# The second expert stage in plain float32: 96 slots in three lots of 32, four column groups

## The chip, the cores and the metric

The kernel runs on one core of a Trainium2 chip. The metric is the device time of one execution in microseconds (us), the median of three runs. A measurement of this kernel tells a change from none from about 0.2% on. Engines are named as in the profile: PE is TensorE, PEld its weight loads, DVE is VectorE, ACT is ScalarE, SP is SyncE, which issues nearly all DMAs.

## The reference, cut to what matters

256 tokens of width 1024 pass a first block (mixers and 32 experts) and a second block of two layers. The last layer ends with a mixture of 8 experts, two per token, and a per-layer embedding. The change is in this mixture:

```python
def swiglu(x, w1, w3, w2):
    return (jax.nn.silu(x @ w1) * (x @ w3)) @ w2

def moe_swiglu(x, router_w, router_b, w1, w3, w2):
    logits = (x @ router_w + router_b).astype(jnp.float32)
    top_v, top_i = lax.top_k(logits, TOP_K)                  # TOP_K = 2 of N_EXPERTS_2 = 8
    top_p = jax.nn.softmax(top_v, axis=-1)
    gate = jnp.sum(jax.nn.one_hot(top_i, N_EXPERTS_2, dtype=jnp.float32) * top_p[..., None], axis=-2)
    gate = gate.astype(x.dtype)
    out = jnp.zeros_like(x)
    for e in range(N_EXPERTS_2):
        out = out + gate[..., e:e + 1] * swiglu(x, w1[e], w3[e], w2[e])
    return out
```

x is 256x1024 in float32, w1 and w3 are 1024x2816 for each expert, w2 is 2816x1024. That is 8 x 3 x 1024 x 2816 x 4 bytes = 276.8 MB of weights. With the given inputs the reference sends 81, 47, 76, 46, 65, 81, 65 and 51 tokens to the eight experts.

## The kernel before, in words

**Streaming.** SP streams all weights of the kernel, in the order of use, into a ring of nine pieces (RAW = 9) of at most 2048 floats on each of 128 partitions, 1 MB. `stream` (L535) lets piece n go only when piece n - 9 is used up (semaphore `used`, incremented by the last matmul on a piece).

**Precision.** In most stages a weight piece is first split in two fp32r parts: ACT casts it to an upper part (`split_high`, L657, into `high_parts`), DVE subtracts to get the lower part in place (`split_low`, L661). The left operand is split too, and each product takes three fp32r matmuls (`matmul3`, L624 to L626; `lower_last`, L634, L635, L638). The first expert stage (moe1, `pairs_pe`, L2748) does otherwise: it multiplies the raw float32 pieces, with two experts of 64 slots each side by side as two column groups of 64 columns of the array (L2830, L2845).

**The second expert stage (moe2, `moe_main_pe`, L2368, with `moe_main_act` and `moe_main_dve`).** Each expert has one bucket of 128 slots; four buckets make a group (TOGETHER = 4). DVE makes one-hot selections (L2642), PE gathers the rows of a group with them (L2374, L2377), gathers each slot's gates, and turns the selections. The width 2816 is walked in steps of 512 and one of 256: 6 steps an expert, 48 in all. A step has four up pieces (two of w1, two of w3; 4 rows of 512 floats a partition) and two down pieces (2 rows of w2 of 1024 floats), so the stage has 264 MB-pieces in 280 DMAs. For a step PE does up (L634, L635, L638; banks 2 and 3), ACT the silu (L2584), DVE the product with the gate (L2676), PE turns the hidden block (L2425), ACT and DVE evacuate it in two parts (L2559, L2661), PE does down (L624 to L626; banks 0 and 1). down of a step is issued behind up of the next. After an expert ACT and DVE take its result in two parts (L2566, L2665), PE scatters it to the tokens in four quarters (L2439, L2440), DVE adds them to x (L2682). For the last expert the two halves of the columns are taken one after the other (L2627, L2736, L2629, L2738), so that the first half is out before the last matmuls are done.

**What stands around it.** Before the stage: the output projection of the mixer, the router and its norm; the ring already holds the first nine pieces of moe2, and ACT and DVE have split three of them. After it: `ple_part(1)` with five pieces, then the final norm and the stores. If an expert has more tokens than its cap (128 before), `rest_pe` and its like run a general loop (`overfull`); otherwise they are jumped over.

## Time and profile before

| | |
|---|---|
| median of 3 runs (lowest, highest) | 2231.16 us (2228.6, 2231.96) |
| the profiled execution | 2228.87 us |
| its span, first to last instruction | 2227.1 us |
| PE, PEld, DVE, ACT busy | 94%, 70%, 62%, 50% of the span |
| bytes moved | 617.42 MB, mean 277 GB/s |

The page's section 2 cuts the span in 40 slices of 55.7 us, each digit tenths of busy time. The first expert stage fills slices 7 to 14, the second slices 26 to 39. Durations of matmuls are modelled and overlap; the pace of a stretch is read from starts: (start of the last minus start of the first) over the count.

### The profile page before, as it was taken

The page shows a single profiled execution, that of the slowest core. Times are in us where ns is not written, and L with a number is a line of the kernel's source. Part 1 is how long each engine was busy: PE and PEld are TensorE (multiplying, and loading weights), DVE is VectorE, ACT ScalarE, POOL GpSimd, SP SyncE. Part 2 cuts the span into 40 slices and gives each one's busy share as a digit, 9 for nine tenths or more (in the row PEclk, how much of TensorE's full clock was granted, in tenths as well). Part 3 has the DMA queues.
Part 4 walks back from the last instruction along what each step waited for, and adds up shares of the span by engine and source line. Part 5 has one row for each costly group of instructions (what it writes and reads, how often), then busy time and mean ns, then how long its engine had stood idle before and what let it go on. Part 6 is the DMA issues. An engine that isn't in the chain of part 4 may idle for free.

```text
span 2227.1 us, 28497 instructions
## 1 busy us (share of the span) xinstructions
PE 2095.3 (94%) x11674; PEld 1548.8 (70%) x11674; DVE 1369.9 (62%) x1689; ACT 1113.0 (50%) x1267; POOL 24.9 (1%) x35
## 2 busy tenths in 40 slices
PE   9999989889777889999999989999999999999997
PEld 7678873234222258778888877888888888888885
DVE  8766661011000037765546767888898888989886
ACT  6545431000000035564336546667777676777765
POOL 1000000000000000100000010000000000000000
PEclk9999999999999999999999999999999999999999
DMA  9754448999999986165555522699999989999991
GB/s 224 199 151 152 152 142 349 421 422 421 421 421 421 421 316 223 36 209 183 170 175 189 168 78 91 245 364 359 368 357 365 363 294 363 358 372 357 367 358 47
DMA packets 281497, 617.42 MB, mean 277 GB/s; under 512 B 31880, under 2 KB 130440, under 8 KB 243984
## 3 DMA queue, kind: packets, MB, share of 16 engines
q1 hardware_dynamic: 279952, 611.85, 76.4%
q10 hardware_dynamic: 1408, 3.67, 0.4%
q8 instruction: 95, 1.56, 0.3%
q14 instruction: 42, 0.34, 0.1%
HBM read 612.34 MB, written 1.05 MB: 275 GB/s over the span
## 4 chain that ended last, share of the span: by engine, by line
PE 74%; DMA 15%; DVE 6%; ACT 3%; issue 1%; SPq 0%; POOL 0%; DVEq 0%; ACTq 0%; POOLq 0%
PE ps L634 9%; PE ps L635 9%; PE ps L638 9%; PE ps L624 8%; PE ps L626 8%; PE ps L625 8%; DMA ring<-in_w_up 5%; DMA ring<-in_w_down 5%; DMA ring<-in_w_gate 4%; PE ps L2830 4%; PE ps L2845 1%; DVE ring_parts L661 1%; ACT high_parts L657 1%; PE ps L2040 1%; PE ps L2047 1%
## 5 line engine op out<-in xcount | busy, mean ns | idle before, releaser
L661 DVE TENSOR_TENSOR ring_parts<-ring,high_parts 128x2048 fp32r<-128x2048 f32 (+2 forms) x382 | 854.7, 2272 | 127.0 <-ACT high_parts L657 126.0
L657 ACT CAST high_parts<-ring 128x2048 fp32r<-128x2048 f32 (+2 forms) x382 | 716.8, 1899 | 101.0 <-PE ps L626 53.7
L626 PE MATMUL ps<-high_parts,arena_parts 128*128 128x512 f32 (+1 forms) x860 | 339.4, 395 | 0.0
L2830 PE MATMUL ps<-ring,arena 128*64 128x512 f32 x1024 | 232.4, 596 | 51.6 <-DMA ring<-in_w_up 26.6
L634 PE MATMUL ps<-high_parts 128*128 128x512 f32 x528 | 208.6, 395 | 0.0
L2830 PEld LDWEIGHTS ps<-ring,arena 128*64 128x64 f32 x1024 | 80.1, 136 | 184.7 <-issue 184.5
L635 PE MATMUL ps<-high_parts 128*128 128x512 f32 x528 | 206.1, 390 | 0.0
L624 PE MATMUL ps<-high_parts,hT_parts 128*128 128x512 f32 (+1 forms) x480 | 195.0, 406 | 0.0
L626 PEld LDWEIGHTS ps<-high_parts,arena_parts 128*128 128x128 f32 x860 | 162.0, 188 | 39.0
L625 PE MATMUL ps<-ring_parts,hT_parts 128*128 128x512 f32 (+1 forms) x480 | 188.4, 392 | 0.0
L634 PE MATMUL ps<-high_parts,hT_parts 128*128 128x512 f32 (+1 forms) x448 | 176.9, 396 | 0.8 <-ACT arena L1360 0.8
L624 PE MATMUL ps<-high_parts,arena_parts 128*128 128x512 f32 x380 | 150.9, 397 | 1.6 <-DVE arena_parts L2661 1.0
L625 PE MATMUL ps<-ring_parts,arena_parts 128*128 128x512 f32 x380 | 150.6, 396 | 0.0
L3002 DVE SCALAR_TENSOR_TENSOR arena<-ps,arena 128x512 f32<-128x512 f32 x16 | 12.0, 750 | 215.6 <-PE ps L2830 199.1
L638 PE MATMUL ps<-ring_parts,high_parts 128*128 128x512 f32 x528 | 141.5, 390 | 0.0
L2845 PE MATMUL ps<-ring,arena 128*64 128x512 f32 x512 | 116.5, 596 | 26.1 <-DMA ring<-in_w_down 25.4
L2918 ACT COPY arena<-ps 128x512 f32<-128x512 f32 x16 | 9.4, 586 | 252.3 <-PE ps L2797 252.3
L638 PE MATMUL ps<-ring_parts,hT_parts 128*128 128x512 f32 (+1 forms) x448 | 119.7, 389 | 0.7 <-DVE ring_parts L661 0.7
L638 PEld LDWEIGHTS ps<-ring_parts,high_parts 128*128 128x128 f32 x528 | 99.1, 188 | 21.2
L634 PEld LDWEIGHTS ps<-high_parts 128*128 128x128 f32 x528 | 99.5, 189 | 19.9
L635 PEld LDWEIGHTS ps<-high_parts 128*128 128x128 f32 x528 | 99.2, 188 | 20.2
L635 PE MATMUL ps<-high_parts,arena_parts 128*128 128x512 f32 (+1 forms) x292 | 113.0, 388 | 0.0
(615 smaller groups left out, 2776.9 us busy)
## 6 DMA issues: line engine op xcount, KB each, us to landing
ring<-in_moe_w SPq DMA_DIRECT2D x248, 1024.0 KB, 5.5
ring<-in_w_gate SPq DMA_DIRECT2D x64, 1024.0 KB, 16.1
ring<-in_w_up SPq DMA_DIRECT2D x64, 1024.0 KB, 16.1
ring<-in_w_down SPq DMA_DIRECT2D x64, 1024.0 KB, 16.6
ring<-in_w_in SPq DMA_DIRECT2D x104, 256.0 KB, 4.7
ring<-in_ffn_w SPq DMA_DIRECT2D x44, 512.0 KB, 4.9
ring<-in_w_in SPq DMA_DIRECT2D x20, 1024.0 KB, 5.8
ring<-in_moe_w SPq DMA_DIRECT2D x32, 512.0 KB, 5.0
```

The source lines that it names most:

```text
L624: pe.matmul(dst, a_hi, b_hi, start=first, stop=False, skip_group_check=True)
L625: pe.matmul(dst, a_hi, b_lo, start=False, stop=False, skip_group_check=True)
L626: return pe.matmul(dst, a_lo, b_hi, start=False, stop=last, skip_group_check=True)
L634: pe.matmul(dst, x_hi, w_hi, start=first and i == 0, stop=False, skip_group_check=True)
L635: pe.matmul(dst, x_lo, w_hi, start=False, stop=False, skip_group_check=True)
L638: mm = pe.matmul(dst, x_hi, w_lo, start=False, stop=last and i == len(x) - 1, skip_group_check=True)
L657: act.copy(high_flat(p), raw_flat(p)).then_inc(upper, 1)
L661: dve.tensor_tensor(raw_flat(p, ring_parts_flat), raw_flat(p), f32(high_flat(p)), ALU.subtract).then_inc(split, 1)
L2040: pe.matmul(ps[:, 2 * t + h, :], x_hidT[:, t, c, :], a[:, c, cols], start=(k == 0 and c == 0), stop=False, skip_group_check=True)
L2047: mm = pe.matmul(ps[:, 2 * t + h, :], x_hidT_lo[:, t, c, :], a[:, c, cols], start=False, stop=(k == f.steps - 1 and c == FB // P - 1), ski ...
L2830: mm = pe.matmul(ps[rows, bank, :], pair_rows[r][:, c0 + i, q * P + a * HALF:q * P + (a + 1) * HALF], w[a][:, i, :], start=(c0 + i == 0), ...
L2845: mm = pe.matmul(ps[rows, half, :], pair_hidT[:, c, rows], w[a][:, i, half * 512:(half + 1) * 512], start=(st.j == 0 and c == 0), stop=(st ...
```

## The change

`plan_moe` and `moe_main_*` go; `plan_wide`, `wide_pe`, `wide_act` and `wide_dve` come for moe2:

- The cap is 96 slots an expert, as three lots of 32 (LOTS, SPAN). Selections, gathered rows and turned selections are 384 wide instead of 512.
- No piece of moe2 is split, in the stage or ahead of it, and nor are the gathered rows and the hidden block. Matmuls take the raw float32 ring.
- A step is 1024 wide (the last of an expert 768): 3 steps an expert, 24 in all, with eight up pieces (2 rows of 1024 or 768 floats a partition) and four or three down pieces. There are 280 DMAs as before: 216 of 1 MB, 64 of 768 KB.
- In `up` and `down` the stationary operand is 128x32 (a lot), the moving one 256 or 192 columns. Four matmuls in a row take the four quarters of the 1024 columns, each in its own column group of the array, so a piece has 2 x 3 x 4 = 24 matmuls. Lot g's gate half and up half lie in bank 2 + g.
- The hidden block is turned by DVE in 32x32 blocks (`dve.transpose`), not by PE. The gate no longer goes into the hidden block: it scales the result, in twelve instructions of 32x256 (six on ACT, six on DVE), which also bring the quarters into rows of slots. `gates` therefore makes every slot's gates on all four column groups (96 small matmuls for a group of four experts).
- The result of the last expert is no longer taken in halves during its last matmuls; both engines wait for the last piece.

The diff, its core:

```diff
 PAIRS, HALF = NE1 // 2, P // 2
+LOTS, SPAN = 3, 96
...
+        def plan_wide(name, w1, w3, w2, gain_row):
...
+            f.subs, f.e, f.cap, f.passes, f.buckets = NE2, 1, SPAN, 2, NE2
+            f.base, f.plan = dict(moe_before), []
+            f.rows_before = KC
...
+            starts = range(0, DFF, 1024)
+            for b in range(f.buckets):
+                rows = w2[b]
+                for k, c0 in enumerate(starts):
+                    st = Step()
+                    st.bucket, st.c0, st.n, st.since = b, c0, min(1024, DFF - c0), k
...
+            def down(st):
+                rows = w2[st.bucket][st.c0:st.c0 + st.n].rearrange("(p c) n -> p c n", p=P)
+                return [new_piece([(0, PIECE, rows[:, c:c + 2, :])]) for c in range(0, st.n // P, 2)]
+
             for s, st in enumerate(f.plan):
                 st.own, st.no = s + 1, f.base["step"] + s + 1
-                st.up = gu_pieces_of(f, st.e, st.c0, st.n)
+                cols = slice(st.c0, st.c0 + st.n)
+                st.up = [new_piece([(0, 2 * st.n, w[st.bucket][:, c:c + 2, cols])]) for w in (f.w1, f.w3) for c in range(0, KC, 2)]
                 if s:
-                    q = f.plan[s - 1]
-                    q.down = down_pieces_of(f, w2, q.e, q.c0, q.n)
-            q = f.plan[-1]
-            q.down = down_pieces_of(f, w2, q.e, q.c0, q.n)
-            first = 0
-            for s, st in enumerate(f.plan):
-                if st.first:
-                    first = s
-                st.since = s - first
+                    f.plan[s - 1].down = down(f.plan[s - 1])
...
-            if half and f is moe2:
-                act.wait_ge(used, pieces_of["out_1_2"][-1].n + 1)
-                split_high(act, f.plan[0].up[2])
...
-                pe.wait_ge(split, p.k)
-                a, b = high_of(p, D), low_of(p, D)
...
-                    mm = matmul3(pe, ps[:, half, :], m_hidT[:, c, :], m_hidT_lo[:, c, :], a[:, i, cols], b[:, i, cols],
-                                 st.first and c == 0, st.last and c == st.n // P - 1)
...
+            def gates(r):
+                for c in (KC - 2, KC - 1):
+                    rows_ready(pe, f, r, c)
+                for q in range(TOGETHER):
+                    for g in range(LOTS):
+                        at, e = SPAN * q + 32 * g, TOGETHER * r + q
+                        for t in range(NT):
+                            for s in range(4):
+                                mm = pe.matmul(ps[32 * s:32 * s + 32, 5, 6 * q + 2 * g:6 * q + 2 * g + 2], f32(wide_sel[:, t, at:at + 32]),
+                                               gate_w[:, t, 2 * e:2 * e + 2], start=(t == 0), stop=(t == NT - 1), skip_group_check=True)
+                mm.then_inc(sig("moe_gates_psum"), 1)
...
+            def up(st, i):
+                p, r, q = st.up[i], st.bucket // TOGETHER, st.bucket % TOGETHER
+                off, n = (0, 256)[i // 4], st.n // 4
+                pe.wait_ge(piece_ready[p.slot], p.ready)
+                w = raw_flat(p).rearrange("p (c n) -> p c n", n=st.n)
+                for k in range(2):
+                    c = 2 * (i % 4) + k
+                    if st.first and q == 0 and i < 4:
+                        rows_ready(pe, f, r, c)
+                    for g in range(LOTS):
+                        x_rows = wide_rows[r][:, c, q * SPAN + 32 * g:q * SPAN + 32 * g + 32]
+                        for s in range(4):
+                            mm = pe.matmul(ps[32 * s:32 * s + 32, 2 + g, off:off + n], x_rows, w[:, k, s * n:(s + 1) * n],
+                                           start=(i == 0 and k == 0), stop=(i % 4 == 3 and k == 1), skip_group_check=True)
+                mm.then_inc(used, 1)
+
+            def down(st, i):
+                p = st.down[i]
+                if i == 0:
+                    pe.wait_ge(sig("moe_hidT"), st.no)
+                    if st.first and st.bucket:
+                        pe.wait_ge(sig("moe_y"), base + st.bucket)
+                pe.wait_ge(piece_ready[p.slot], p.ready)
+                w = raw_flat(p).rearrange("p (c n) -> p c n", n=D)
+                hidT = wide_hidT[st.no % 2][:, 0:LOTS * st.n // 4].rearrange("p (g j t) -> p g j t", g=LOTS, t=32)
+                final = st is f.plan[-1] and i == len(st.down) - 1
+                for k in range(2):
+                    j = 2 * i + k
+                    for g in range(LOTS):
+                        for s in range(4):
+                            mm = pe.matmul(ps[32 * s:32 * s + 32, g // 2, g % 2 * 256:g % 2 * 256 + 256], hidT[:, g, j, :],
+                                           w[:, k, 256 * s:256 * s + 256], start=(st.first and j == 0 and g != 1),
+                                           stop=(st.last and j == st.n // P - 1), skip_group_check=True)
+                            if final and (k, g, s) == (1, LOTS - 1, 1):
+                                mm.then_inc(sig("moe_half_done"), 1)
+                mm.then_inc(used, 1)
+
+            held = None
...
+                if held:
+                    pe.wait_ge(sig("moe_hid"), held.no)
+                for i in range(8):
+                    up(st, i)
+                    if i == 3 and s == 0:
+                        pe.wait_ge(*ended("moe2_gates"))
+                        gates(0)
+                    if i == 3 and k == 0 and b == TOGETHER - 1:
+                        gates(1)
+                    if 2 <= i < 6 and k == 1 and b:
+                        scatter(b - 1, i - 2)
+                    if i == 5 and k == 1 and b % TOGETHER == 0:
+                        turn_sel(b // TOGETHER)
+                if held:
+                    for i in range(len(held.down)):
+                        down(held, i)
+                if k == 2 and b == TOGETHER - 2:
+                    gather(1)
+                held = st
...
+            def result(b):
+                act.wait_ge(used, f.plan[3 * b + 2].down[-1].n + 1)
+                act.wait_ge(sig("moe_scattered"), 4 * (base + b))
+                for s in range(2):
+                    for g in range(LOTS):
+                        ins = act.mul(wide_y[32 * g:32 * g + 32, 256 * s:256 * s + 256],
+                                      ps[32 * s:32 * s + 32, g // 2, g % 2 * 256:g % 2 * 256 + 256],
+                                      wide_gate[32 * s:32 * s + 32, wide_scale(b, g, 0)])
+                astep(act, ins)
+                ins = act.copy(m_yh[0:SPAN, 0:512], wide_y[0:SPAN, 0:512])
+                ins.then_inc(*((sig("moe_half_upper"), 1) if b == f.buckets - 1 else (sig("moe_y_upper"), 1)))
+                act.wait_ge(sig("wide_y"), b + 1)
...
+            def silu(st):
+                act.wait_ge(used, st.up[-1].n + 1)
+                if st.own > 1:
+                    act.wait_ge(sig("moe_hid"), st.no - 1)
+                n = st.n // 4
+                for g in range(LOTS):
+                    ins = act.activation(wide_sg[:, g * n:g * n + n].rearrange("p (j i) -> p j i", i=32),
+                                         ps[:, 2 + g, 0:n].rearrange("p (i j) -> p j i", i=32), ACT.Silu,
+                                         scale=wide_gate[:, wide_scale(st.bucket, g, 1)])
+                ins.then_inc(sig("moe_silu"), 1)
...
+                for s in range(2, 4):
+                    for g in range(LOTS):
+                        ins = dve.tensor_scalar(wide_y[32 * g:32 * g + 32, 256 * s:256 * s + 256],
+                                                ps[32 * s:32 * s + 32, g // 2, g % 2 * 256:g % 2 * 256 + 256],
+                                                wide_gate[32 * s:32 * s + 32, wide_scale(b, g, 0)], None, ALU.mult)
+                ins.then_inc(sig("wide_y"), 1)
...
+            def product(st):
+                dve.wait_ge(used, st.up[-1].n + 1)
+                dve.wait_ge(sig("moe_silu"), st.no)
+                if st.own > 1:
+                    dve.wait_ge(sig("moe_hidT"), st.no - 1)
+                n = st.n // 4
+                hid, hidT = wide_hid[:, 0:LOTS * n], wide_hidT[st.no % 2][:, 0:LOTS * n]
+                dve.tensor_tensor(hid.rearrange("p (g j i) -> p g j i", g=LOTS, i=32),
+                                  ps[:, 2:2 + LOTS, 256:256 + n].rearrange("p g (i j) -> p g j i", i=32),
+                                  wide_sg[:, 0:LOTS * n].rearrange("p (g j i) -> p g j i", g=LOTS, i=32), ALU.mult)\
+                    .then_inc(sig("moe_hid"), 1)
+                dve.wait_ge(sig("moe_hid"), st.no)
+                dve.transpose(hidT, hid).then_inc(sig("moe_hidT"), 1)
...
-                    if l and i == 1:
-                        act.wait_ge(used, pieces_of[name][1].n + 1)
-                        split_high(act, moe2.plan[0].up[0])
-                        split_high(act, moe2.plan[0].up[1])
...
-            stage_moe(moe2),
+            stage_wide(moe2),
```

`select`, `gather`, `turn_sel`, `scatter`, `rows`, `gate`, `add` and the order of `wide_act` and `wide_dve` follow `pairs_*` and `moe_main_*`, with 96 for 128.

## Rows read from the trace of the kernel before

**Rows 1.** The page: busy time, and the span in 40 slices.

```profile
PE 2095.3 (94%) x11674; PEld 1548.8 (70%) x11674; DVE 1369.9 (62%) x1689; ACT 1113.0 (50%) x1267; POOL 24.9 (1%) x35
...
PE   9999989889777889999999989999999999999997
...
GB/s 224 199 151 152 152 142 349 421 422 421 421 421 421 421 316 223 36 209 183 170 175 189 168 78 91 245 364 359 368 357 365 363 294 363 358 372 357 367 358 47
```

**Rows 2.** Waits of PE, 1420 to 2181 us: us, times, longest.

```profile
PE ps L624 <- DVE arena_parts L2661: 1.0, 1, 1.0
PE ps L624 <- DVE ring_parts L661: 0.6, 1, 0.6
```

**Rows 3.** Groups by form, 1400 to 2227 us: count, busy us, mean ns.

```profile
L661 DVE TENSOR_TENSOR ring_parts<-ring,high_parts 128x2048 fp32r<-128x2048 f32 x267 | 597.3, 2284 | 18.1 <-ACT high_parts L657 18.1
L657 ACT CAST high_parts<-ring 128x2048 fp32r<-128x2048 f32 x266 | 501.2, 1915 | 58.8 <-PE ps L638 37.0 <-PE ps L626 21.8
...
L2584 ACT ACTIVATE arena<-ps,arena 128x256 f32<-128x256 f32 x8 | 3.8, 476 | 10.3 <-PE ps L638 10.3
```

**Rows 4.** Timeline of PE, first up piece: start us, us, form, count.

```profile
1403.57 0.39 PE L634 MATMUL ps<-high_parts,hT_parts 128*128 128x512 f32 x1
...
1406.31 0.39 PE L634 MATMUL ps<-high_parts,hT_parts 128*128 128x512 f32 x1
```

**Rows 5.** Timeline of PE, float32 product in four column groups (L3763).

```profile
922.90 1.50 PE L3763 MATMUL ps<-ring,arena 128*32 128x128 f32 x44
```

**Rows 6.** The same line: ns min, median, max.

```profile
L3763 PEld LDWEIGHTS ps<-ring,arena x128: 106/110/110, 922.9 to 1323.3; 128*32 128x32 f32 x128
L3763 PE MATMUL ps<-ring,arena x128: 272/273/297, 922.9 to 1323.4; 128*32 128x128 f32 x128
```

**Rows 7.** Timeline of PE in the first expert stage, a pair of pieces.

```profile
537.37 3.65 PE L2830 MATMUL ps<-ring,arena 128*64 128x512 f32 x16 [0.66 <-DMA ring<-in_w_up]
```

**Rows 8.** Busy time by stretch: us, engines, granted clock, DMA share, GB/s.

```profile
1420.00:2180.00 760.00, 758.30 (x3394) 624.91 (x3393) 660.65 (x407) 544.10 (x379) 0.00 (x0) 1.00 0.98 354
520.00:760.00 240.00, 193.71 (x852) 71.79 (x850) 22.03 (x29) 14.86 (x21) 0.00 (x0) 1.00 1.01 421
1415.00:1419.00 4.00, 4.00 (x28) 3.61 (x27) 0.00 (x0) 0.00 (x0) 0.00 (x0) 1.00 1.05 398
```

**Rows 9.** Timelines, first expert stage: SP first reissue, PE last pair.

```profile
342.05 1.33 SPq L535 DMA_DIRECT2D ring<-in_w_gate  x2
...
802.36 3.65 PE L2845 MATMUL ps<-ring,arena 128*64 128x512 f32 x16 [1.28 <-DMA ring<-in_w_down]
```

**Rows 10.** Timeline of PE before and in the gather of the second stage.

```profile
1392.02 0.40 PE L1763 MATMUL ps<-r_pairs,causal_up 128*128 128x16 f32 x2 [1.75 <-DVEq L1932]
...
1394.18 0.79 PE L2374 MATMUL ps<-arena_parts 128*128 128x512 f32 x1
...
1395.20 0.63 PE L2374 MATMUL ps<-arena_parts 128*128 128x512 f32 x1
1395.63 0.63 PE L2377 MATMUL ps<-arena_parts 128*128 128x512 f32 x1
...
1399.12 0.41 PE L2374 MATMUL ps<-arena_parts 128*128 128x512 f32 x1
1399.36 0.40 PE L2377 MATMUL ps<-arena_parts 128*128 128x512 f32 x1
```

**Rows 11.** Timeline of PE at the second stage's end.

```profile
2181.54 0.40 PE L626 MATMUL ps<-high_parts,arena_parts 128*128 128x512 f32 x1
2181.99 0.50 PE L2439 MATMUL ps<-arena_parts 128*128 128x512 f32 x1
```

**Rows 12.** Timelines of DVE, then ACT, at the second stage's end.

```profile
2181.24 0.69 DVE L2736 TENSOR_TENSOR arena_parts<-ps,arena_parts 128x512 fp32r<-128x512 f32 x1 [2.50 <-ACT arena_parts L2627]
...
2183.20 2.47 DVE L2682 TENSOR_TENSOR x<-x,ps 128x512 f32<-128x512 f32 x4
...
2185.93 1.58 ACT L820 ACTIVATE hT_parts<-ps,l_gT 128x256 fp32r<-128x256 f32 x4
```

More of the change, by code:

```diff
@@ L433, in plan_moe @@
+            moe_before["group"] += f.buckets // TOGETHER
             f.until = order["piece"]
             f.adds = 4 * moe_before["bucket"]
-            f.subs, f.cap, f.passes = buckets, P, 1
-            plan_rest(f, width)
+            plan_rest(f, DFF)
             return f
@@ L1963, in emit @@
         lot = [MX.take(PIECE) for _ in range(HIGH)]
-        moe2.group.high = [lot[k] for k in (2, 1, 0, 3, 4)]
         MX = Arena(arena)
@@ L1967, in emit @@
         pair_rows = [MX.take(KC, TOGETHER * P) for _ in range(2)]
+        MX.at = HI_AT
+        wide_rows = [MX.take(KC, TOGETHER * SPAN) for _ in range(2)]
+        wide_sg, wide_hid = MX.take(LOTS * 256), MX.take(LOTS * 256)
+        wide_hidT = [MX.take(LOTS * 256) for _ in range(2)]
+        wide_y = MX.take(D)
         assert MX.at <= HI_END
+        wide_gate = arena[:, MR_AT:MR_AT + 48]
+        wide_sel = m_sel.rearrange("p t n -> p (t n)")[:, 0:NT * TOGETHER * SPAN].rearrange("p (t n) -> p t n", t=NT)
         MX.at = MR_AT + MR_SIZE + 1024
@@ new lines, in wide_scale, with wide_act, rows, gate @@
+        def wide_scale(b, g, what):
+            at = 24 * (b // TOGETHER) + 6 * (b % TOGETHER) + 2 * g + what
+            return slice(at, at + 1)
+        def wide_act(act, f):
+            base = f.base["bucket"]
+            def rows(r):
+                for c in range(0, KC, 2):
+                    act.wait_ge(sig("moe_gathered"), KC * (f.base["group"] + r) + c + 1)
+                    act.copy(wide_rows[r][:, c, :], ps[:, 5 + c % 3, 0:TOGETHER * SPAN]).then_inc(sig("moe_rows_upper"), 1)
+            def gate(r):
+                act.wait_ge(sig("moe_gates_psum"), f.base["group"] + r + 1)
+                act.copy(wide_gate[:, 24 * r:24 * r + 24], ps[:, 5, 0:24]).then_inc(sig("moe_gates"), 1)
+            def result(b):
[10 more added lines that the diff above has]
+                act.wait_ge(sig("wide_y"), b + 1)
+                act.copy(m_yh[0:SPAN, 512:D], wide_y[0:SPAN, 512:D]).then_inc(sig("moe_y_upper"), 1)
+            def turned_sel(r):
+                act.wait_ge(sig("moe_sel_turned"), f.base["group"] + r + 1)
+                act.copy(m_selT[0:SPAN].rearrange("p b s -> p (b s)"), ps[0:SPAN, 5:7, :].rearrange("p a b -> p (a b)"))\
+                    .then_inc(sig("moe_selT"), 1)
+            def silu(st):
[8 more added lines that the diff above has]
+                ins.then_inc(sig("moe_silu"), 1)
+            router_exp_act(act, f)
+            rows(0)
+            for s, st in enumerate(f.plan):
+                b, k = st.bucket, st.since
+                if s == 1:
+                    ahead = act.mark_branch_hint_location()
+                if k == 0 and b == TOGETHER - 1:
+                    rows(1)
+                    gate(1)
+                if s == 0:
+                    gate(0)
+                if k == 1 and b:
+                    result(b - 1)
+                if k == 1 and b % TOGETHER == 0:
+                    turned_sel(b // TOGETHER)
+                if s == 0:
+                    act.wait_ge(sig("moe_gates"), f.base["group"] + 1)
+                if k == 0 and b == TOGETHER:
+                    act.wait_ge(sig("moe_gates"), f.base["group"] + 2)
+                silu(st)
+            rest_act(act, f, ahead)
+            result(f.buckets - 1)
+            rows_upper(act, 1)
+            split_until(act, "act", group_ple[1], 1)
@@ L3043, in moe_gained_dve, with stage_wide @@
+        def stage_wide(f):
+            return (lambda pe: wide_pe(pe, f)), (lambda act: wide_act(act, f)), (lambda dve: wide_dve(dve, f)), no_pool
         def moe_gained_dve(dve, f, half):
```

495 lines of the change are left out of this document (129 added, 366 removed).

## The prediction

> **What bounds the kernel now.** I read the page first, then the stage of the change by stretches, then its waits, then its timelines. The page shows PE at 94% and GB/s at 421 in slices 7 to 13 but near 360 in slices 26 to 38 [rows 1]. So the first expert stage runs at the speed of the DMAs and the second does not. The stretches say the same: from 1420 to 2180 us PE is busy 758.3 of 760 us at a granted clock of 1.00 and 354 GB/s flow; from 520 to 760 us 421 GB/s flow and PE has gaps [rows 8]. In the second stage PE waited 1.6 us in all [rows 2]. The splits on DVE (597 us from 1400 us on) and ACT (501 us) are large, but PE never stands for them, so taking them away is worth nothing by itself [rows 3]. What sets the end there is the pace of PE: the first up piece takes 1403.57 to 1406.31, 2.74 us for 12 matmuls [rows 4]. A piece of 1 MB at 421 GB/s takes 2.49 us. The stage runs from 1403.57 us to the last down matmul, which ends at 2181.94 us [rows 4, 11], 778.4 us for 276.8 MB, where 421 GB/s would need 657 us.
>
> **PE after.** A piece gets 24 matmuls of 128x32 by 256 columns. The nearest form is L3763: raw float32 of the ring, 128x32 stationary, 128 columns, four column groups in turn. 44 of them take 1.50 us [rows 5], the last being 0.27 us long [rows 6], so (1.50 - 0.27) / 43 = 28.6 ns each, 114 ns for four. The first expert stage has 16 matmuls of 512 columns in two column groups in 3.65 us, at most 456 ns a pair [rows 7]. Both give 0.89 ns a column with all groups at work. Four of 256 columns are then 228 ns, 57 ns each, and a piece 24 x 57 = 1.37 us, against 2.74. A bound below is the 28.6 ns of [rows 5] (0.7 us), one above is serial work, taken up under the rivals. At 1.37 us PE is far ahead of a piece every 2.49 us. The stage turns from PE to the DMAs, as the first expert stage is.
>
> A page of the Trainium skill speaks against this: "FP8 and Floating Point Precision", TensorE Precision Notes, has true FP32 take four passes through the array. By it 256 columns cost 1024 cycles, 427 ns for four, and a piece would need 2.56 us, just over a DMA's pace. The trace disagrees: by four passes a pair of 512 columns would be 853 ns, and [rows 7] has 456 at most.
>
> **DMAs after.** All nine slots are free or filling, since PE waits for data. SP starts to refill when the first piece is used. Nine of the 280 pieces lie in the ring by then. Of the rest 119 are up pieces of 1 MB in rows of 4 KB, 64 are of 768 KB in rows of 3 KB, 88 are down pieces in rows of 8 KB. The first expert stage has rows of 8 KB at 421 GB/s [rows 8]. That is 311 ns a row on each of 16 DMA engines. In the second stage, in a short stretch with only up pieces in rows of 2 KB, 398 GB/s flow [rows 8], 82 ns a row. Between them by a straight line, 4 KB take 158.6 ns (413 GB/s, 2.54 us a piece) and 3 KB 120.5 ns (408 GB/s, 1.93 us). Sum: 119 x 2.538 + 64 x 1.928 + 88 x 2.491 = 302.0 + 123.4 + 219.2 = 644.6 us. The bounds are 421 GB/s throughout (635 us) and the worse of the 2 KB figures, 354 GB/s of the long stretch, for all up pieces (about 703 us; but there PE held the DMAs back, so I take the line). The first expert stage shows what is lost beside this: from SP's first refill at 342.05 to PE's last pair at 802.36 are 460.3 us [rows 9], where 183 pieces at 2.49 make 455.8. The difference, 4.5 us, is the way from issue to landing and small gaps; I add it.
>
> **Start.** The gather before the stage takes 1394.18 to 1403.57, 9.4 us [rows 4, 10]. With 384 columns for 512 it is three quarters, 7.0 us, and PE starts up at 1401.2. The selection ahead of it is on DVE and only gets narrower. The splits that fall away from ACT and DVE before the router are not what the gather waits for; I give them nothing. SP's first refill is at 1401.2 + 1.4 = 1402.6. The 96 gate matmuls stand behind the fourth piece, 2.7 us at 28.6 ns; the ring and the queue ahead hide them, as they hide the second gather (about 6 us), the turned selections (2 us) and the scatters (64 matmuls of 0.24 us in the whole stage). None of these holds PE longer than the some 20 us that eight pieces in flight cover. If that cover were gone, they would cost some 30 us together.
>
> **End.** The last piece can be used at 1402.6 + 644.6 + 4.5 = 2051.7, its matmuls end 1.6 us later, 2053.3. Before this was 2181.94: 128.6 us gained. Behind it the change adds. Before, the first half of the result was ready by then: the scatter starts at 2181.99 and the adds at 2183.20 [rows 11, 12]. After, ACT must do six products of 32x256 and a copy, and DVE a subtraction. The nearest row is four 128x256 activations in 1.58 us, 0.39 us each [rows 12], so 2.35 + 0.6 + 0.7 and two hand-overs make 3.8 us; a bound below is 2 us (half the rows' time, being 32 partitions), one above 6 us (the 0.48 us of the silu [rows 3] and slow hand-overs). Of these 3.8 the second half saves about 0.6, as its subtraction follows at once. I take +3.2 us. The five pieces of the last embedding are no longer in the ring when the stage ends; they land some 3 to 15 us after the last piece, while the scatters, the turning of x and its norm run, so they stay hidden, with a few us at risk.
>
> **Other parts.** The silu is three instructions of 128x256, 0.48 us each [rows 3], then a product of 768 elements a row (1 to 1.5 us by the 0.69 us of 512 elements [rows 12]) and the turn in 32x32 blocks, which no row shows: between 0.5 and 5 us. The next up waits only for the product, about 3 us after the last up piece. Four down pieces, 10 us of data, lie between. The turn is needed another eight pieces later. So all of it is worth 0. The waits of `result` on ACT stand ahead of a silu, but a whole up lies before that silu's data. The cap of 96 is not reached: the fullest expert has 81 tokens, so the general loop stays out.
>
> **Sum.** 128.6 - 3.2 = 125.4 us. The profiled execution of 2228.87 us becomes 2103.5; the median of the runs, 2231.16, lies 2.3 higher and becomes **2106 us**. Bounds of the unknown terms: DMA 421 throughout, -10; the up rows at 398 instead of 413 and 408, +16; more if slots are refilled in bursts; the tail -2 to +10. Own range 2090 to 2135.
>
> **Rivals.**
> - *A matmul costs about 108 ns, not 57.* Either float32 costs nearly twice what I read, or the clock falls from 2.4 to 1.2 GHz because PE now stands half of the time. For it: at 1395.20 matmuls that later come every 0.24 us come every 0.43 [rows 10], after PE stood 1.75 us; that is 1.8 times; the new gaps are 1.1 us after each 1.4 us of work. Against it: gaps of 0.66 us leave the granted clock at 1.00 [rows 7, 8]. PE's work: 264 MB-pieces x 24 x 0.108 = 684 us and 30 of the small work, from 1401.2 to 2115, so 62 us over the forecast: 2168 us.
> - *Slower: weight loads don't overlap.* Each matmul brings its own load of 128x32, 110 ns long [rows 6]. Place: the 6720 matmuls of `up` and `down`. From 111 ns a matmul on the kernel gets slower (the 778 us of the stage less 30, over 6720). Load and matmul end to end are 164 ns: about 1100 us for the stage, some 2560 us in all; loads alone one after the other, 770 us, 2223. Against it: in [rows 5] four matmuls, with four loads of 110 ns, take 114 ns, so loads of different groups do overlap. The Trainium skill, "TensorE: Matmul & The Clock Gate", Part 3, says that loads overlap running matmuls only where the row group differs, and here all share the rows; by that rule this rival is the forecast, at 164 ns. [Rows 5] shows the same layout without such a stall.
> - *The DMAs stay at the old pace.* With 4 KB rows no better than 354 GB/s the stage needs 58 us more: 2164. Against it: 398 in a short stretch with shorter rows.
> - *The change does not do what it says*: the general loop runs for an expert over 96. With 81 at most it can't; it would cost hundreds of us.
>
> **How the numbers follow.** Forecast 0.77; matmul of 108 ns 0.08; DMAs at the old pace 0.06; other stalls of 30 to 60 us 0.03; weight loads 0.05 (nearly all slower); general loop 0.01. A measurement tells 0.2% from no change. Faster: 0.77 + 0.08 + 0.06 + 0.03 = 0.94; slower 0.05; same 0.01. The own range leaves a little out on both sides; with part of the two middle rivals (a clock or a rate that fails for part of the stage) I set 2090 to 2150.
>
> **What would show it.** Stretches from 1420 to 2040 us at 412 to 416 GB/s; PE waiting for the DMAs in most pieces; 24 matmuls of a piece starting within 1.4 us; SP's waits gone to the landing side, with landings near 20 us; the last piece's matmuls at 2052 us; 48 us from there to the end. Wrong would be matmuls every 108 ns or more, a granted clock under 0.9, GB/s under 400 with PE waiting, or a wait of PE for `moe_hid` or `moe_y`.

## The result, and the profile after

The changed kernel takes 2198.76 us (median of four runs, 2195.8 to 2200.63) against 2231.56 of the kernel before beside it: a ratio of 0.985, interval 0.9835 to 0.987. So it is faster, by 33 us and not by the 125 us forecast. The sign was right, the size was not, and 2199 lies outside the range of 2090 to 2150.

The profiled execution took 2200.63 us with a span of 2198.8. Its page has these lines: busy time of each engine, PE and GB/s in 40 slices, and the DMA queue that the profile names `instruction` (transfers, MB, share of the engines' time).

```profile
PE 2051.8 (93%) x22118; PEld 1415.1 (64%) x22118; DVE 789.4 (36%) x1408; ACT 615.3 (28%) x1009; POOL 24.9 (1%) x35
...
PE   9999989879777889999999999999999999999997
...
GB/s 221 200 147 147 155 161 305 421 421 421 421 422 421 421 359 271 4 203 171 172 187 196 155 98 78 152 307 412 369 385 350 320 403 369 408 382 377 412 363 68
...
q8 instruction: 176, 2.88, 0.5%
```

Beside [rows 1], DVE fell from 1370 to 789 us and ACT from 1113 to 615. PE fell only from 2095 to 2052 and is still full in every slice of the stage. The GB/s touch 412 in two slices and lie mostly under it. The number of PE instructions went up from 11674 to 22118. The forecast had 24 matmuls a piece, 6720 in the stage. The groups of PE by form, 1400 to 2150 us (count, busy us, mean ns, idle us before), show another number:

```profile
L2744 PE MATMUL ps<-ring,arena 128*32 128x256 f32 x6144 | 349.9, 384 | 6.7 <-DVE arena L2924 3.7 <-issue 3.0
L2762 PE MATMUL ps<-ring,arena 128*32 128x256 f32 x4224 | 235.0, 379 | 0.5 <-issue 0.5
L2744 PE MATMUL ps<-ring,arena 128*32 128x192 f32 x3072 | 127.6, 326 | 1.5 <-issue 1.5
```

`up` (L2744) has 128 pieces of 1 MB with 24 matmuls each, 3072, and the trace has 6144. `down` (L2762) has 88 x 24 = 2112, and the trace has 4224. **One plain float32 matmul is two records.** The timeline of PE at the stage's start (start us, us, form, count) gives the pace:

```profile
1403.25 0.40 PE L2676 MATMUL ps<-arena_parts 128*128 128x384 f32 x1
1403.58 10.57 PE L2744 MATMUL ps<-ring,arena 128*32 128x256 f32 x192
1413.97 0.90 PE L2702 MATMUL ps<-gate_w,arena_parts 128*32 128x2 f32 x83
1415.54 1.05 PE L2702 MATMUL ps<-gate_w,arena_parts 128*32 128x2 f32 x107 [0.68 <-issue]
```

Four pieces take 1403.58 to 1413.97, 10.4 us: 192 records every 54 ns, or 96 matmuls every 108 ns, 2.60 us a piece. The forecast had 1.37 us for it, the kernel before 2.74 [rows 4]. The waits of PE in the stage and just behind it, 1395 to 2165 us (total us, times, longest), hold no DMA:

```profile
PE ps L2744 <- issue: 4.6, 4, 3.0
PE ps L2702 <- issue: 4.5, 2, 3.8
PE ps L2728 <- DVE arena_parts L2909: 4.4, 1, 4.4
PE ps L2744 <- DVE arena L2924: 3.7, 1, 3.7
PE ps L2711 <- DVE x L2934: 0.8, 1, 0.8
```

And the stretches (us, busy us of PE, PEld, DVE, ACT, POOL, granted clock, DMA share, GB/s):

```profile
1420.00:2140.00 720.00, 708.69 (x13389) 489.44 (x13392) 95.07 (x138) 60.46 (x136) 0.00 (x0) 0.99 0.97 370
...
1500.00:1520.00 20.00, 20.00 (x380) 14.34 (x375) 0.00 (x0) 0.44 (x2) 0.00 (x0) 1.00 1.02 412
```

In the whole stage 370 GB/s flow, against 354 in [rows 8]. Where only up and down pieces run, it is 412. The last `down` ends at 2147.68 us. So the stage is 744.1 us long, where it was 778.4; the rest up to the span's end is 51.1 us, where it was 45.2 (2227.1 less 2181.9).

### The profile page after: what moved, and what is told of

Read it like the earlier page. It is cut to its first block, busy times and chain, and to the rows that moved or that the text cites. A ratio compares the mean times of both kernels' runs of the same rounds, so it can differ in the third digit from the quotient of the medians.

```text
span 2198.8 us, 48386 instructions
## 1 busy us (share of the span) xinstructions
PE 2051.8 (93%) x22118; PEld 1415.1 (64%) x22118; DVE 789.4 (36%) x1408; ACT 615.3 (28%) x1009; POOL 24.9 (1%) x35
## 4 chain that ended last, share of the span: by engine, by line
PE 73%; DMA 15%; DVE 6%; ACT 3%; issue 2%; SPq 0%; POOL 0%; DVEq 0%; ACTq 0%; POOLq 0%
PE ps L2744 21%; PE ps L2762 10%; DMA ring<-in_w_up 5%; DMA ring<-in_w_down 5%; PE ps L622 5%; PE ps L624 5%; PE ps L623 5%; DMA ring<-in_w_gate 4%; PE ps L2451 4%; PE ps L632 2%; PE ps L633 2%; PE ps L636 2%; PE ps L2466 1%; PE ps L2041 1%; PE ps L2048 1%
## 5 line engine op out<-in xcount | busy, mean ns | idle before, releaser
L2744 PE MATMUL ps<-ring,arena 128*32 128x256 f32 (+1 forms) x9216 | 477.6, 365 | 8.3 <-issue 4.6
L2744 PEld LDWEIGHTS ps<-ring,arena 128*32 128x32 f32 x9216 | 328.2, 111 | 148.1 <-issue 21.1
L659 DVE TENSOR_TENSOR ring_parts<-ring,high_parts 128x2048 fp32r<-128x2048 f32 (+2 forms) x118 | 264.2, 2245 | 108.1 <-ACT high_parts L655 107.2
L2762 PE MATMUL ps<-ring,arena 128*32 128x256 f32 x4224 | 235.0, 379 | 0.5 <-issue 0.5
L655 ACT CAST high_parts<-ring 128x2048 fp32r<-128x2048 f32 (+2 forms) x118 | 219.3, 1864 | 39.4 <-PE ps L624 29.1
L2762 PEld LDWEIGHTS ps<-ring,arena 128*32 128x32 f32 x4224 | 154.6, 110 | 74.6 <-issue 1.3
L624 PE MATMUL ps<-high_parts,arena_parts 128*128 128x512 f32 (+1 forms) x508 | 199.9, 393 | 0.0
L622 PE MATMUL ps<-high_parts,hT_parts 128*128 128x512 f32 (+1 forms) x480 | 194.7, 406 | 0.0
L623 PE MATMUL ps<-ring_parts,hT_parts 128*128 128x512 f32 (+1 forms) x480 | 188.3, 392 | 0.0
L633 PE MATMUL ps<-high_parts,arena_parts 128*128 128x512 f32 (+1 forms) x292 | 113.0, 388 | 0.0
L632 PE MATMUL ps<-high_parts,hT_parts 128*128 128x512 f32 (+1 forms) x272 | 107.4, 396 | 0.8 <-ACT arena L1358 0.8
L622 PEld LDWEIGHTS ps<-high_parts,hT_parts 128*128 128x128 f32 x480 | 90.7, 189 | 21.1 <-issue 2.2
L623 PEld LDWEIGHTS ps<-ring_parts,hT_parts 128*128 128x128 f32 x480 | 90.6, 189 | 18.8
```

What stands on the lines that cost most here:

```text
L622: pe.matmul(dst, a_hi, b_hi, start=first, stop=False, skip_group_check=True)
L623: pe.matmul(dst, a_hi, b_lo, start=False, stop=False, skip_group_check=True)
L624: return pe.matmul(dst, a_lo, b_hi, start=False, stop=last, skip_group_check=True)
L632: pe.matmul(dst, x_hi, w_hi, start=first and i == 0, stop=False, skip_group_check=True)
L633: pe.matmul(dst, x_lo, w_hi, start=False, stop=False, skip_group_check=True)
L655: act.copy(high_flat(p), raw_flat(p)).then_inc(upper, 1)
```

## The experiments

The theory after the result (A): TensorE still sets the pace, since a float32 matmul costs 108 ns here and the small work between the pieces comes on top of it. The rival (B): the DMAs, now close to their bound, set it. The first four kernels tell these apart.

**Matmuls alone.** A program with one line for each kind of matmul, operands in SBUF, no DMA while it runs:

```diff
+for k in range(48):          # L51, and L54 with one group only
+    for s in range(4):
+        pe.matmul(ps[32*s:32*s+32, 1, 0:256], w[:, 0, lot(k)], w[:, 1, 256*s:256*s+256], ...)
+for k in range(48):          # L57 in float32, L60 in fp32r
+    pe.matmul(ps[:, 3, 0:256], w[:, 0, block(k)], w[:, 1, 0:256], ...)
```

> A program of TensorE work alone, on operands that lie in SBUF; it computes nothing of the reference. Blocks of matmuls, each with a line of its own: after a warm-up, 192 plain float32 matmuls (128x32 stationary by 256 columns) dealt over the four column groups; 48 of the same in one group; 48 of 128x128 by 256 in float32; the same in the rounded type; 128x128 by 512 in the rounded type; 192 with 2 columns in four groups; then groups of 24 float32 matmuls with 2 or with 4 matmuls of 96x128 by 512 in the rounded type after them. Theory A, two records for each float32 matmul at the pace that the changed kernel shows: the first block shows 384 records at 54 ns, 20.8 us, and the groups work side by side, so the second takes four times as long for each matmul (430 ns, 48 in 20.7 us), and so does 128x128 by 256 in float32; the rounded type takes a quarter of that (108 ns), and 512 columns 215 ns. The changed form then costs as much for 96 slots (3 lots x 4 groups x 108 ns = 1.30 us for a chunk of 128x1024 weights) as the form before did for 128 (3 parts x 2 x 215 = 1.29 us). Theory B, a matmul is one record of 54 ns and the rest of the time is waiting: 192 records in 10.4 us. A change between the two forms costs 0.2 to 0.3 us each way by the scatters' rows in the changed kernel; the rival is that it costs nothing and the scatters were waiting for something else.

Its timeline of PE (start us, us, form, count, idle before):

```profile
24.87 20.93 PE L51 MATMUL ps<-w 128*32 128x256 f32 x384
45.61 20.88 PE L54 MATMUL ps<-w 128*32 128x256 f32 x96
66.43 20.99 PE L57 MATMUL ps<-w 128*128 128x256 f32 x96
87.06 6.10 PE L60 MATMUL ps<-r 128*128 128x256 f32 x48
93.00 11.07 PE L63 MATMUL ps<-r 128*128 128x512 f32 x48
104.00 2.30 PE L67 MATMUL ps<-w 128*32 128x2 f32 x255
108.90 1.89 PE L67 MATMUL ps<-w 128*32 128x2 f32 x128 [2.61 <-issue]
...
119.09 2.80 PE L72 MATMUL ps<-w 128*32 128x256 f32 x48
121.82 0.73 PE L74 MATMUL ps<-r 96*128 96x512 f32 x2
122.48 2.80 PE L72 MATMUL ps<-w 128*32 128x256 f32 x48
```

All float32 lines show two records a matmul, the rounded type (fp32r) one. 192 matmuls in four groups take 20.7 us (24.87 to 45.61), 108 ns each; 48 in one group take 20.8 us, 434 ns each. So the groups do run side by side, four times as fast. But the full 128x128 form in float32 takes 430 ns, no more than the one group (L57), and fp32r 124 ns for the same 256 columns (L60) and 229 ns for 512 (L63), where 108 and 215 were expected. Per block of 128x1024 weights the new form costs 3 lots x 4 groups x 108 = 1.30 us, the old one 3 parts x 2 x 229 = 1.37 us. **Three quarters of the slots at four times the work of one rounded pass is three passes again: the change trades three for three.** Expected were 1.30 and 1.29.

The period of the last lines is 122.48 - 119.09 = 3.39 us. Without 2.60 for the float32 part and 0.46 for two fp32r matmuls, 0.33 us are left: a change of form and back costs that.

The two-column matmuls (L67) start some 8 ns apart for 255 records; then PE pauses 2.6 us with no releaser, though no weights flow here, and 128 records later 2.1 us more. With the pauses the 384 records take 8.9 us (104.00 to 112.90), 23 ns each. **The traces say what these pauses end with.** In this program a transfer of 16 KB in the queue `instruction` starts at 106.55 us and one at 110.50, and PE goes on at 108.90 and 112.90, 2.4 us after each. In the stage of the change it is the same: such transfers at 1413.33, 1418.72 and 1699.16 us, PE goes on at 1415.54, 1420.93 and 1701.54. In the traces of the change, its repetition and four of its variants below (all but two lots) there are 32 places in the stage where PE starts nothing for over 0.45 us with no releaser, and each ends 2.2 to 2.6 us after the start of such a transfer; with the two here it is 34 of 34. The transfers come every 6.7 us in the stage, so chance would hardly do it. On the average one of them brings 125 records with their weight loads (22118 records, 176 transfers); at 54 ns a record these last 6.8 us, at 8 ns 1 us. So PE very likely waits for its own instructions, which many tiny matmuls use up faster than they come; no experiment changes the supply of instructions alone.

The Trainium skill, "FP8 and Floating Point Precision", TensorE Precision Notes, counts four passes for true FP32, and this agrees: 434 ns is 3.8 times the 114 ns that half a matmul of 512 columns has (229 / 2), and 3.5 times the 124 ns of 256 columns. It is the rule that the prediction set aside. The skill's "TensorEngine Tiling (Array Packing)", Key Properties, says that a change of the tiling mode drains the engine. The 0.33 us are what a change of form and back costs here; the forms differ in data type and in the size of the stationary operand too, and no run tells how much of it is the drain.

**Two lots of three.** Only the range of the loop over the lots in `up` and `down` is changed, from 3 to 2.

```diff
-                    for g in range(LOTS):
+                    for g in range(2):
```

> The changed kernel without the third lot's matmuls in up and down: slots 64 to 95 of each expert are not computed. Everything else, the transfers too, stays. Theory A (TensorE at 48 records of 54 ns a piece, 2.60 us, sets the pace): a piece falls to 32 records, 1.73 us, under the 2.55 us in which the 16 queues bring 1 MB at 412 GB/s. The stage of 744 us then becomes that of the transfers, 276.8 MB at 412 GB/s = 672 us and a few us of start: 2125 to 2140 us. Theory B (the transfers set the pace already, TensorE only waits for them): no gain, 2190 to 2201 us. If the small work between the pieces (scatters, gates, gather, the first wait for VectorE) were added to either, the gain would be under 45 us.

2132.83 us, ratio to before 0.956 (0.9547 to 0.9579): 66 to 67 us under the change. That is A, and B is out. PE now waits for the DMAs as the forecast said of the change itself (waits of the whole span, then two stretches):

```profile
PE ps L2744 <- DMA ring<-in_moe_w: 69.3, 119, 2.1
PE ps L2762 <- DMA ring<-in_moe_w: 49.1, 74, 2.2
```

```profile
1420.00:1440.00 20.00, 16.29 (x280) 10.38 (x276) 1.94 (x2) 2.48 (x4) 0.00 (x0) 0.94 0.85 301
...
1520.00:1560.00 40.00, 30.76 (x568) 17.02 (x561) 3.58 (x5) 2.24 (x6) 0.00 (x0) 1.00 1.02 410
```

This kernel is what I had forecast: a TensorE ahead of its data. Its stage lasts 675 us, from 1404.76 us, where 652.1 were forecast. The rate was nearly right, 409 to 412 GB/s for 413. But in the first 35 us only about 290 flow, since PE stands 4.7 us at the gates and 3.7 us in the second step, which costs some 10 us. From 1440 to 2080 us the mean is 408, where the forecast's sum (267.4 MB in 644.6 us) stands for 415; that is 11 more. So even with the pace that I took, the forecast was some 23 us too low in the stage.

**Half the data.** Each piece brings one of its two chunks, and both products use that one:

```diff
-... w[st.bucket][:, c:c + 2, cols] ...     rows[:, c:c + 2, :]     w[:, k, ...]
+... w[st.bucket][:, c:c + 1, cols] ...     rows[:, c:c + 1, :]     w[:, 0, ...]
```

> The changed kernel with half of every weight piece of the second expert stage left out: the transfer brings one of a piece's two chunks, and TensorE uses it twice, so its matmuls are the same in number and form and half of the weights is not used. Theory A (TensorE sets the pace): the stage keeps its length but for the few places where TensorE waits for a piece, 2185 to 2200 us. Theory B (the transfers set it): the stage loses far more than 50 us, 2150 us and below. Between them: if both are close to the bound and disturb each other (a late piece now and then), 10 to 25 us are gained.

2190.31 us, ratio 0.982 (0.9804 to 0.9836). A again: half of 277 MB gone, and 8 to 10 us gained. PE keeps its load at half the flow:

```profile
1600.00:1800.00 200.00, 197.06 (x3736) 129.49 (x3729) 28.88 (x42) 18.05 (x42) 0.00 (x0) 0.98 0.62 183
```

The pace of the matmuls does not change: 48 records of `up` in a row take 2.59 us in the median of this trace, and of the change's. Start to start, pauses of over 0.7 us left out, the records of `up` sum to 452.8 us, in the change to 454.1 and in its repetition to 455.7. What shrinks is PE's waits without a releaser, in `up` and `down` and at the gates: 5.3 us for 9.6 (10.6 in the repetition). They make up about half of the gain. The rest lies in many small places, and the same kernel's stage differs by 3 us between two executions (744.1 and 747.2 us; here 737.3).

**One transpose of four, in the kernel before.** This asks where the 33 us come from.

```diff
-                for c in range(nc_):
+                for c in range(1):
```

> The kernel before with one of the four transposes of hidden values on TensorE in each step of the second expert stage (48 of 176; the other three quarters of the hidden values are not turned). It measures what taking TensorE's transposes away is worth there. Theory A (TensorE was the bound before, and the change gained by taking them off it): 27 us for all by the sum of their rows, 128 of 176 are 20 us: 2208 to 2214 us. Rival (they lay beside waits for the split weights): 2225 to 2232 us.

2214.55 us, ratio 0.9927 (0.991 to 0.9943): 16 us for 128 of the 176 transposes. That is A's side, just above its 2208 to 2214, since the gain was to be 20 us. By proportion all 176 are worth 22 us. They lay on PE's path, so taking them off it is a real part of what the change gained.

The next four were measured side by side. They test the remaining terms: if TensorE sets the pace, each small piece of work on it must be worth its length.

**The change again.**

> The changed kernel as it is, on the same chip as the next three, so that they can be set against it: 2196 to 2201 us.

2200.30 us, ratio 0.9861 (0.9846 to 0.9876). In its trace the stage starts at 1401.78 us and lasts 747.2 us, against 1403.58 and 744.1 in the first trace of the same kernel. So a term of 1 to 3 us, read from one trace, is not sure.

**Gates in two steps.**

```diff
-                for q in range(TOGETHER):
-                    for g in range(LOTS):
-                        for t in range(NT):
-                            for s in range(4):
-                                mm = pe.matmul(ps[32 * s:32 * s + 32, 5, 6 * q + 2 * g:6 * q + 2 * g + 2], ...)
+                for q in range(TOGETHER):
+                    for t in range(NT):
+                        mm = pe.matmul(ps[0:SPAN, 5, 32 + 2 * q:34 + 2 * q], f32(wide_sel[:, t, q * SPAN:(q + 1) * SPAN]), ...)
+            # ACT copies the 96x8 values to gate_rows; two pieces later:
+                for g in range(LOTS):
+                    for s in range(4):
+                        mm = pe.matmul(ps[32 * s:32 * s + 32, 5, 8 * g:8 * g + 8], ident[0:SPAN, 32 * g:32 * g + 32],
+                                       gate_rows[0:SPAN, 8 * r:8 * r + 8], start=True, stop=True, ...)
```

> The changed kernel with its gate values dealt in two steps: 8 matmuls bring the values of all 96 slots of four experts (96 stationary columns, 2 moving), ScalarE copies them to SBUF, and 12 matmuls with rows of the identity lay them out for the four column groups, two pieces later: 20 matmuls for 96, twice in the stage. Theory A (what TensorE issues is what counts, since it sets the pace): the gates' records, 8.2 us each time, and the two pauses of 3.4 and 4.0 us beside them without a releaser fall to 1 to 2 us each time: 14 to 20 us gained, 2179 to 2185 us. Rival (the pauses are the queues' catching up, the transfers take the time back): 5 us or less, 2193 to 2197 us.

2188.07 us, ratio 0.981 (0.9796 to 0.9823): 12.2 us under the change. The rival's 5 us or less is out, and A's 14 to 20 was a little too much. The timelines of PE at the second group's gates, first of the changed kernel, then of this one:

```profile
1696.06 1.65 PE L2702 MATMUL ps<-gate_w,arena_parts 128*32 128x2 f32 x173
1701.54 0.43 PE L2702 MATMUL ps<-gate_w,arena_parts 128*32 128x2 f32 x18 [3.83 <-issue]
```

```profile
1689.11 1.52 PE L2701 MATMUL ps<-gate_w,arena_parts 128*96 128x2 f32 x16
1690.56 5.39 PE L2751 MATMUL ps<-ring,arena 128*32 128x256 f32 x96
1695.76 0.35 PE L2709 MATMUL ps<-arena,ident 96*32 96x8 f32 x24
```

The old form holds PE from 1696.06 to 1701.8, 5.7 us, of which 1.7 are records running. In the new one the steps take 1.45 us and 0.2, with no pause behind them. The small matmuls are a fifth, so their instructions are too, which fits the waits for instructions. About 4 us are gained at each of the two gates, 8 together; the remaining 4 are smaller pauses of about 1 us in `up` and `down`, of which the trace now has fewer. The expectation was too high because its 8.2 us "each time" are, read again, the starts of both gates together, with two of the three pauses in them.

**Scatters in two lots.**

```diff
-                    if 2 <= i < 6 and k == 1 and b:
-                        scatter(b - 1, i - 2)
+                    if i in (2, 4) and k == 1 and b:
+                        for part in ((0, 1, 2) if i == 2 else (3,)):
+                            scatter(b - 1, part)
```

> The changed kernel with the scatters of an expert in two lots (three ahead of up piece 2's successor, one two pieces later) where it has four lots of one. Theory A: each change from matmuls in four groups to full ones and back costs 0.33 us (the program of matmuls alone: 3.39 us for 24 float32 matmuls of 2.60 and two of 0.23), two of them less in each of 7 experts: 4.6 us gained, 2193 to 2197 us. Rival (three scatters in a row wait for VectorE's results and for its additions): no gain, or 1 to 3 us slower.

2194.24 us, ratio 0.9842 (0.9829 to 0.9856): 6.1 us under the change, 4.6 expected. The intervals of the two ratios overlap, so the size is rough; the mechanism stands in the timelines. The change (first fence) has 3.39 us from one scatter to the next, as the matmuls alone had. In this kernel (second fence) the scatters follow one another with no change of form between them:

```profile
1534.98 0.50 PE L2728 MATMUL ps<-arena_parts 96*128 96x512 f32 x1
1535.31 0.40 PE L2729 MATMUL ps<-arena_parts 96*128 96x512 f32 x1
1535.64 2.80 PE L2744 MATMUL ps<-ring,arena 128*32 128x256 f32 x48
1538.37 0.50 PE L2728 MATMUL ps<-arena_parts 96*128 96x512 f32 x1
```

```profile
1533.60 0.50 PE L2728 MATMUL ps<-arena_parts 96*128 96x512 f32 x1
1533.93 0.39 PE L2729 MATMUL ps<-arena_parts 96*128 96x512 f32 x1
1534.17 0.39 PE L2728 MATMUL ps<-arena_parts 96*128 96x512 f32 x1
1534.40 0.40 PE L2729 MATMUL ps<-arena_parts 96*128 96x512 f32 x1
```

**Both, and the turned selection earlier.** Beside the two edits above:

```diff
-                    if i == 5 and k == 1 and b % TOGETHER == 0:
-                        turn_sel(b // TOGETHER)
+                    if i == 5 and k == 1 and b == TOGETHER:
+                        turn_sel(1)
+                if s == 0:
+                    turn_sel(0)
```

> Both together, and the turning of the first four experts' selection moved from the second step into the wait of 4 us that TensorE has after the first step's up pieces, for VectorE's product. Theory A: the gains of the two add up, 19 to 25 us, and the move hides some 1.6 us: 2173 to 2181 us. Rival (the transfers at 672 us for the stage come into sight and take a part): 2181 to 2188 us.

2179.63 us, ratio to before 0.9766 (0.9753 to 0.978): 20.7 us under the change. The two gains (12.2 and 6.1) and 1 to 2 us of the move add up within 2 us. The wait in the second step shrinks from 3.7 to 2.7 us, and the stretch carries 381 GB/s for 370:

```profile
PE ps L2753 <- DVE arena L2942: 2.7, 1, 2.7
```

```profile
1420.00:2130.00 710.00, 705.60 (x13376) 479.92 (x13368) 93.83 (x139) 60.75 (x139) 0.00 (x0) 1.00 0.99 381
```

It is the fastest kernel here that computes everything, 51 us under the one before.

## Why the prediction was wrong, point by point

**What bounds the kernel now: right.** PE set the pace before; the transposes' removal alone gave its 16 us.

**The pace of a matmul: the step that failed.** I took 44 records of L3763 in 1.50 us for 44 matmuls and 16 records in [rows 7] for 16 matmuls. They are 22 and 8. The counts of the kernel before, held against the code, would have told. Its first stage issues 8 matmuls for two pieces in `up`, 512 for 128 pieces, and L3763 stands in a loop that runs 64 times:

```profile
L2830 PE MATMUL ps<-ring,arena x1024: 592/592/644, 338.4 to 785.7; 128*64 128x512 f32 x171
```

[Rows 6] has x128 for those 64, and the fp32r line L634 in [rows 4] one record a matmul. With 8 matmuls, four pairs, in 3.65 us, a pair costs 912 ns, not 456. Four passes gave 853 by the prediction's own estimate. So [rows 7] were said to speak against the page and in truth agreed with it. The term was 1.37 us a piece and measured 2.60. The piece is then slower than its transfer (2.49 to 2.54 us), and the bound stays where it was.

**The first rival was the case.** It had 108 ns a matmul, the measured value, and 684 us for the pieces. The trace agrees: 10368 records at 54 ns and 3072 of 192 columns at three quarters of it are 560 + 124 = 684 us. Its time was 2168, 31 us too low, and it had 0.08 of the chances. Of its two reasons it is the first, the cost of float32. The clock is not it: granted 1.00 in the stretch at 412 GB/s. What it missed is the small work, for which it had 30 us; the trace has 744.1 - 684 = 60 us between 1403.58 and 2147.68. The main parts, from the differences of starts: 28 scatters at 0.79 us, 22 us; the two gates with the pauses in and behind them, 12 us; the second gather, 8 us; the changes between `up` and `down`, 72 at 0.07 us, 5 us; the wait for the first product, 4 us; the turned selections, 3 us; three more pauses of about 1 us, 3 us. That is 57; 3 us are spread too thin to name.

**"The ring and the queue ahead hide them": failed with the first step.** Eight pieces in flight cover a pause of PE only if PE is faster than the DMAs. With PE as the bound each microsecond of small work costs one, as the gates and the scatters show.

**The DMAs: right where they could be seen.** 412 GB/s for 413 with rows of 4 KB. The sum of 644.6 us with 4.5 on top was some 23 us short in the kernel with two lots: about 10 in the first two steps, and 11 since 408 GB/s flow on the average of the rest. One bound was added up wrong: 354 GB/s for all up pieces (175.1 MB) with 219.2 us for the others is 714 us, not 703, so the rival of the old pace would have been at 2175. Nothing else hangs on it.

**Start: 2.4 us off.** The gather takes 8.4 us (1395.14 to 1403.58) where 7.0 were forecast. It shrank with its columns only at the start, where the granted clock is 0.52: 0.32 us a matmul for the 0.43 of [rows 10]. At a granted clock of 1.00 it keeps its pace: 0.24 us at 512 columns before and 0.24 at 384 now (1403.01 to 1403.25). Something other than the columns sets that pace; I did not test what. The other 1.0 us is that the gather began later, at 1395.14 for 1394.18; in the repetition it began at 1393.33, so this is scatter between executions.

**End: 5.9 us for 3.2.** The hand-over after the last `down` is 4.4 us instead of 3.8 less 0.6. The six products take 0.465 us each on ACT, one starting every 0.48, where I had 0.39. And PE stood meanwhile, so it does the scatters at half its clock (0.43 us a matmul for 0.23), in the stretch 2151 to 2159 us:

```profile
2147.77 2.98 DVE L2901 TENSOR_SCALAR arena<-ps,arena 32x256 f32<-32x256 f32 x6 [15.45 <-PE ps L2762]
2151.31 0.69 DVE L2909 TENSOR_TENSOR arena_parts<-arena,arena_parts 96x512 fp32r<-96x512 f32 x1 [0.55 <-ACT arena_parts L2829]
...
2151.00:2159.00 8.00, 6.95 (x26) 5.97 (x27) 5.63 (x8) 4.59 (x8) 0.00 (x0) 0.57 0.17 66
```

**Silu, product and turn: right**, but for the first step, where no `down` lies between. The turn in 32x32 blocks takes 0.98 us for 768 elements, inside 0.5 to 5.

**The rival of the weight loads: out.** Loads of 110 ns each run beside records that start every 54 ns, in all four groups. On the full array (L60) loads of 192 ns stand beside matmuls every 124 ns. The rule of the Trainium skill that the prediction quotes for this rival ("TensorE: Matmul & The Clock Gate", Part 3) is not borne out here, neither by the stage nor by the matmuls alone.

**The general loop: out.** From 1400 to 2150 us PE has only the lines of `wide_pe`.

**The balance.** The span went down by 28.3 us, and 125.4 were forecast, so 97.1 are missing. Start 2.4, of which about 1 is scatter; TensorE's 684 us over the 652.1 of the DMAs, 32; the small work of the stage, 60; end 2.7. Together 97.1.

And the gain itself: the product matmuls of the stage were 3168 of fp32r at 0.230 us, 729 us, and are 684, 45 less; the transposes are gone, 22 us. Against that stand dearer scatters (0.79 us a pair for 0.46, 9 us), gates with pauses (12 us for 3), the wait for the first product (4 us), the changes between `up` and `down` (5 us), more small pauses (some 3 us) and the end (6 us), 36 together. That leaves 31 us, and the span shows 28. The trade on the products is nearly even (45 us of 729), and 36 of the 67 us that the change won went into small work of its own.

## What to carry to other kernels

Before a pace is read from a group of records, hold the count of the group against the number of matmuls in the code; here a float32 matmul leaves two records, and the time between two starts is half of what it costs. Plain float32 cost close to four rounded passes here. It took the place of three passes over 128 slots with 96, three quarters of them, and four times three quarters is three: 1.30 us for 1.37. The transposes that fell away with the splits were worth 22 us, and small work of the new form took back 36. Many tiny matmuls cost more than their columns say: count their instructions too. Work that "hides behind the ring" hides only while TensorE is ahead of the data: ask this anew for each rival's pace, since small terms come back all at once when it fails.

## What the runs showed of the hardware

- Plain float32, 256 columns: 430 ns a matmul for 128x128, 434 for 128x32 in one column group, 108 ns each with four groups in turn. fp32r: 124 ns for 256 columns, 229 ns for 512. A float32 matmul is two records of the trace, an fp32r one is one.
- From four-group matmuls to full ones and back: 0.33 us, in the program of matmuls alone and in the kernel.
- Many float32 matmuls of 2 columns in a row (384 records in 8.9 us, 23 ns each) bring pauses of 0.7 to 4.7 us in which PE waits for nothing that the waits show. They came without a flow of weights as well, were shorter at half the flow, and went away at the gates with 20 matmuls for 96. All 34 pauses of over 0.45 us without a releaser, these and the smaller ones in `up` and `down`, end 2.2 to 2.6 us after the start of a 16 KB transfer in the queue `instruction`: they are very likely waits for instructions.
- The clock fell to its lower level, 1.2 GHz, after PE had stood for 3 to 4.4 us: granted 0.57 over 1421 to 1425 us, over 1434 to 1442 us and over 2151 to 2159 us, against 1.00 over 1500 to 1520 us. In the program of matmuls alone it was 0.59 over 112.9 to 120 us, behind pauses of 2.6 and 2.1 us.
- The flow of weights leaves the pace of `up` as it is: 48 records take 2.59 us, in the median, at 370 GB/s and at 193.
